# RWKV inverse: T and its transpose kept as sums in PSUM, seeded by a product with the unit matrix

## The reference, cut to what matters

```python
def _rwkv7_scan(r, w, k, v, a, b, s0):
    def step(s, inp):
        r_t, w_t, k_t, v_t, a_t, b_t = inp
        sa = jnp.einsum('bhvk,bhk->bhv', s, a_t)
        s = s * w_t[:, :, None, :] + sa[..., None] * b_t[:, :, None, :] + v_t[..., None] * k_t[:, :, None, :]
        o = jnp.einsum('bhvk,bhk->bhv', s, r_t)
        return s, o
```

## Time and profile before

| | |
|---|---|
| median of three executions | 2289.26 us |
| span of the profiled execution, first to last instruction | 2287.5 us |
| the three executions' own times | 2285.67, 2289.26, 2289.65 us |
| PE busy | 2230.2 us (97%) |
| DVE busy | 982.6 us (43%) |
| ACT busy | 421.9 us (18%) |
| POOL busy | 556.1 us (24%) |
| PE's share of the chain that ended last | 87% |

### The profile page before, as it was taken

How to read it: one execution, slowest core, us unless ns; L and a number is a source line. 1 busy time by engine, 2 the same in 40 slices (tenths; PEclk the granted TensorE clock), 3 DMA queues, 4 the chain that set the end, 5 groups by cost and what they waited for, 6 DMA issues and landing times.

```text
span 2287.5 us, 47135 instructions
## 1 busy us (share of the span) xinstructions
PE 2230.2 (97%) x20858; PEld 2105.6 (92%) x20858; DVE 982.6 (43%) x1259; ACT 421.9 (18%) x775; POOL 556.1 (24%) x288
## 2 busy tenths in 40 slices
PE   8999999999999999999999999999999999999998
PEld 6899988878888799889999988999999999999997
DVE  5333664747546355254443154445114314412523
ACT  4111313214141211163111032110000000000011
POOL 0232201111011022123333301333333333323331
PEclk9999999999999999999999999999999999999999
DMA  7211201112011083236113134111111111111112
GB/s 282 84 41 42 63 20 55 41 40 68 20 58 38 27 271 133 98 133 254 41 46 120 37 131 156 37 46 46 46 37 46 46 46 39 45 46 46 46 37 87
DMA packets 57711, 171.15 MB, mean 75 GB/s; under 512 B 8416, under 2 KB 24160, under 8 KB 54752
## 3 DMA queue, kind: packets, MB, share of 16 engines
q1 hardware_dynamic: 46816, 143.63, 19.0%
q10 hardware_dynamic: 10752, 25.35, 3.2%
HBM read 140.90 MB, written 28.05 MB: 74 GB/s over the span
## 4 chain that ended last, share of the span: by engine, by line
PE 87%; DVE 5%; DMA 3%; ACT 2%; issue 1%; SPq 1%; POOL 0%; ACTq 0%; DVEq 0%; POOLq 0%
PE ps L380 86%; DMA w_raw<-w 2%; DVE TT L1154 1%; DVE F L1154 1%; SPq L2219 1%; ACT F L1758 1%; DMA vc<-vc 1%; DVE F L1157 0%; DVE F L1160 0%; DVE Sst L1157 0%; ACT L1758 0%; DMA par<-par 0%; POOL w_split L371 0%; DVE Xst L1154 0%; PE ps L1024 0%
## 5 line engine op out<-in xcount | busy, mean ns | idle before, releaser
L380 PE MATMUL ps<-A_s,w_split 128*128 128x364 f32 (+1 forms) x6192 | 1081.6, 332 | 8.2 <-ACT zstg L1758 6.0
L380 PEld LDWEIGHTS ps<-A_s,w_split 128*128 128x128 f32 x6192 | 1029.3, 189 | 35.4 <-issue 12.2
L380 PE MATMUL ps<-B_s,w_split 128*128 128x364 f32 (+3 forms) x4032 | 672.5, 328 | 0.2 <-POOL w_split L371 0.2
L380 PEld LDWEIGHTS ps<-B_s,w_split 128*128 128x128 f32 x4032 | 667.7, 188 | 3.4 <-issue 1.0
L368 POOL CAST w_split<-w_raw 128x1024 fp32r<-128x1024 f32 x142 | 154.0, 1084 | 1685.6 <-PE ps L380 1599.7
L371 POOL TENSOR_TENSOR w_split<-w_raw,w_split 128x1024 fp32r<-128x1024 f32 x142 | 402.0, 2831 | 11.4
L1154 DVE TENSOR_TENSOR F<-ps,F 128x1092 f32<-128x1092 f32 (+3 forms) x52 | 62.8, 1208 | 420.6 <-PE ps L380 420.6
L1758 ACT ACTIVATE B_s<-T 128x1092 fp32r<-128x1092 f32 x32 | 35.9, 1121 | 621.6 <-DVE T L1160 621.6
L1160 DVE SCALAR_TENSOR_TENSOR T<-ps,rsx 128x1092 f32<-128x1092 f32 x32 | 41.5, 1296 | 205.3 <-PE ps L380 197.2
L1154 DVE TENSOR_TENSOR B_s<-T,B_s 128x1092 fp32r<-128x1092 f32 x32 | 105.9, 3309 | 1.1
L1154 DVE TENSOR_TENSOR T<-T 128x1092 f32<-128x1092 f32 x58 | 103.8, 1790 | 1.4 <-ACT T L1758 0.2
(11 more groups left out here) (208 smaller groups left out, 1806.0 us busy)
## 6 DMA issues: line engine op xcount, KB each, us to landing
w_raw<-w SPq DMA_DIRECT2D x144, 512.0 KB, 3.6
z<-zstg SPq DMA_DIRECT2D x83, 182.0 KB, 1.9
F<-z SPq DMA_DIRECT2D x16, 546.0 KB, 7.4
w_raw<-w SPq DMA_DIRECT2D x7, 1024.0 KB, 10.4
kc<-kc SPq DMA_DIRECT2D x7, 1024.0 KB, 4.8
vc<-vc SPq DMA_DIRECT2D x7, 1024.0 KB, 4.9
F<-x SPq DMA_DIRECT2D x8, 546.0 KB, 9.8
Zs<-z SPq DMA_DIRECT2D x16, 273.0 KB, 19.6
```

Of the source, the lines that this page charges most:

```text
L380: return pe.matmul(out, lhsT, rhs, start=start, stop=stop, skip_group_check=skip)
```

## The change

T and its transpose are no longer added up in SBUF. A new step `seed` multiplies both by the unit matrix into banks 3u and 3u+1 in level 1, and every level's product adds onto those sums in PSUM (`start=False`). After each level but the last, DVE copies T out of bank 3u (256 elements instead of 512, and no second operand), and ACT copies the transpose out of bank 3u+1 in every level. The next level's x waits for DVE's copy alone, its increments wait for ACT's too. The product `av` moves from level 1 to level 5 and lands in bank 3u, which is free by then; ACT's copy of it moves along. The mark "av" is gone, so ACT's copy of a finished piece of the gates comes behind the levels. DVE's add of the last level is gone, and `wu` waits for ACT's copy of the transpose and for `av_read`. The samples keep their code, with other counts in the waits (`at_t`) and one wait more in `wu`.

```diff
+            def seed(p, h, u):
+                b0 = 3 * u
+                pe.wait_ge(tk_ready, 2 * q_of(p, h) + 2)
+                for c in range(NB):
+                    cross(bank(b0, NB, C)[:, c, :], TT[u][:, 1, c, :], eye, start=(c == 0), stop=False, skip=True)
+                    last = cross(bank(b0 + 1, NB, C)[:, c, :], TT[u][:, 0, c, :], eye, start=(c == 0), stop=False, skip=True)
+                last.then_inc(lvt, 1)
+
+            def grow(p, h, u, lv):
+                b0 = 3 * u
+                pe.wait_ge(xst_ready, at_lv(p, h, lv))
+                pe.wait_ge(lvt, at_z(p, h, lv - 1))
+                for c in range(NB):
+                    if lv < LEVELS - 1:
+                        cross(bank(b0, NB, C)[:, c, :], TT[u][:, 1, c, :], Xst[u][:, c, :], start=False, stop=False, skip=True)
+                    last = both(bank(b0 + 1, NB, C)[:, c, :], Xst[u][:, c, :], TT[u][:, 1, c, :], start=False, stop=False, skip=True)
+                last.then_inc(yz_done, 1)
...
             def wu(p, h, u, nb, levels):
                 q, b0 = q_of(p, h), 3 * u
-                pe.wait_ge(lvl, at_lv(p, h, levels - 1))
+                pe.wait_ge(av_ready, q + 1)
+                if nb == NB:
+                    pe.wait_ge(lvt, at_z(p, h, levels - 1))
+                else:
+                    pe.wait_ge(lvl, at_t(p, h, levels - 1))
...
                     if lv == 1:
+                        for u in range(2):
+                            seed(p, 2 * g + u, u)
+                    if lv == LEVELS - 1:
                         for u in range(2):
                             av(p, 2 * g + u, u, NB)
-                        mark(p, g, "av")
                     for u in range(2):
-                        yz_level(p, 2 * g + u, u, NB, lv, LEVELS)
+                        grow(p, 2 * g + u, u, lv)
...
-                        for u in range(2):
-                            add_level(p, 2 * g + u, u, NB, lv, LEVELS)
+                        if lv < LEVELS - 1:
+                            for u in range(2):
+                                v.wait_ge(yz_done, at_lv(p, 2 * g + u, lv))
+                                v.tensor_copy(TT[u][:, 0, :, :], bank(3 * u, NB, C)).then_inc(lvl, 1)
...
+            def turned_level(p, h, u, lv):
+                a.wait_ge(yz_done, at_lv(p, h, lv))
+                act(TT[u][:, 1, :, :], bank(3 * u + 1, NB, C), ACT.Copy).then_inc(lvt, 1)
...
-                    reads(MARK[p, g, "av"])
-                    for u in range(2):
-                        av_read(p, 2 * g + u, u, NB)
+                    for lv in range(1, LEVELS):
+                        if lv == LEVELS - 1:
+                            for u in range(2):
+                                av_read(p, 2 * g + u, u, NB)
+                        for u in range(2):
+                            turned_level(p, 2 * g + u, u, lv)
```

More of the change, by code:

```diff
@@ L301, in hybrid_step @@
         d_s0r, d_rst, vm_ready, rs_done, rs_new = (sem(n) for n in ("d_s0r", "d_rst", "vm_ready", "rs_done", "rs_new"))
-        rn_mean, rn_ctr, rn_sq, rn_var, rn_rs, rn_out = (sem(n) for n in
-            ("rn_mean", "rn_ctr", "rn_sq", "rn_var", "rn_rs", "rn_out"))
+        rn_mean, rn_ctr, rn_sq, rn_var, rn_rs, lvt = (sem(n) for n in
+            ("rn_mean", "rn_ctr", "rn_sq", "rn_var", "rn_rs", "lvt"))
         rg_t, rg_f, rg_p, rg_hi, rg_s = (sem(n) for n in ("rg_t", "rg_f", "rg_p", "rg_hi", "rg_s"))
@@ L346, in at_lv, with at_t, at_z @@
             return n + h // 2 * 2 * (LEVELS - 1) + 2 * (lv - 1) + h % 2 + 1
+        def at_t(p, h, lv):
+            n = p * (HALVES * (LEVELS - 2) + SLEVELS - 1)
+            if h == HALVES:
+                return n + HALVES * (LEVELS - 2) + lv
+            return n + h // 2 * 2 * (LEVELS - 2) + 2 * (lv - 1) + h % 2 + 1
+        def at_z(p, h, lv):
+            return (2 * p + h // 2) * 2 * LEVELS + 2 * lv + h % 2 + 1
         NA = SEQ // P
@@ L595, in x_level @@
                 else:
-                    pe.wait_ge(lvl, at_lv(p, h, lv - 1))
+                    pe.wait_ge(lvl, at_t(p, h, lv - 1))
                 for c in range(nb):
@@ L602, in av @@
                 q, b0 = q_of(p, h), 3 * u
-                pe.wait_ge(tk_ready, 2 * q + 2)
+                if nb == 1:
+                    pe.wait_ge(tk_ready, 2 * q + 2)
                 for c in range(nb):
-                    last = cross(bank(b0 + 1, NB, C)[:, c, :], NAR[u][:, 1, c, 0:C], TK[u][:, 4, c, :])
+                    last = cross(bank(b0 + (0 if nb == NB else 1), NB, C)[:, c, :], NAR[u][:, 1, c, 0:C], TK[u][:, 4, c, :])
                 last.then_inc(av_done, 1)
+            def seed(p, h, u):
[14 more added lines that the diff above has]
+                last.then_inc(yz_done, 1)
             def yz_level(p, h, u, nb, lv, levels):
@@ L1298, in add_level @@
                 else:
-                    v.wait_ge(lvl, at_lv(p, h, lv - 1))
+                    v.wait_ge(lvl, at_t(p, h, lv - 1))
                 yz = ps[:, b0:b0 + 2, 0:NB * C].rearrange("p a (n c) -> p a n c", c=C)
@@ L1905, in av_read @@
                 a.wait_ge(av_done, q + 1)
-                act(TK[u][:, 1, 0:nb, :], bank(b0 + 1, NB, C)[:, 0:nb, :], ACT.Copy).then_inc(av_ready, 1)
+                act(TK[u][:, 1, 0:nb, :], bank(b0 + (0 if nb == NB else 1), NB, C)[:, 0:nb, :], ACT.Copy).then_inc(av_ready, 1)
+            def turned_level(p, h, u, lv):
+                a.wait_ge(yz_done, at_lv(p, h, lv))
+                act(TT[u][:, 1, :, :], bank(3 * u + 1, NB, C), ACT.Copy).then_inc(lvt, 1)
             def wu_read(p, h, u, nb):
```

## The result

| | before | after |
|---|---|---|
| median of the runs | 2289.45 us (2285.67 to 2292.88, 8 runs) | 2297.35 us (2292.88 to 2303.21, 8 runs) |
| ratio after/before, 95% interval | | 1.0041 [1.0031, 1.0051] |
| profiled execution, span | 2287.5 us | 2297.1 us |
| granted clock | 0.996 | 0.996 |

The changed kernel is slower by 0.4%, 8 to 10 us. Forecast were +2.6 us and most of the chance on "no difference that can be measured". The sign is the forecast's, the size is three times as large, and the time (2297.35) lies at the upper end of the range of 2284.5 to 2298, beside the slower rival's 2298.

What follows compares the result with a forecast made beforehand. PE was taken to bound the kernel, with the DVE-PE ring of 2.71 us bounding a level; -8.7 + 0.4 + 4.8 + 5.2 + 0.4 + 0.5 = +2.6 us gave 2291.9 us, range 2284.5 to 2298.

Steps and rivals of the forecast that it cites:

- slower rival: Levels 2 to 4: PE's queue bounds the rings, only 0.13 of 0.27 us gained in each; 2298 us, chance 0.20.
- Add becomes copy: Levels 1 to 4: DVE's 686 ns add becomes a 415 ns copy, 0.27 us less in each of 32 rings, -8.7 us.
- rings: One level's cycle of x, mask, increments and add or copy; 2.71 us before, forecast 2.44 in levels 2 to 4.
- ACT takes the transpose: Levels 1 to 4: ACT's 385 ns copy finishes over 1 us before the next increments need it; cost zero.
- the waits: Levels 1 to 4: increments wait for two semaphores instead of one; +0.4 us, bounded by 0 and 1.9.
- The seed: Level 1: 64 rows at 28 ns in av's place delay the increments, +0.6 us a group, +4.8 us in all.
- av to level 5: Level 5: av stands between x1 and the increments in PE's queue, +0.65 us a group, +5.2 us (0 to 7.2).
- the handover: Level 5: handing over from ACT to PE takes longer than from DVE, +0.05 us a group, +0.4 us.
- PE's own stalls: Levels 1 to 5: one 0.6 us stall a group shared over its rows makes the seed's extra rows cost +0.5 us.
- The faster rival: Levels 1 and 5: seed and av mostly fall into PE's 0.86 us of room in a level; 2284 us, chance 0.13.

Runs made afterwards that it cites:

- experiment 4: Kernel before with only av moved to level 5: ratio 0.9999; changed kernel without seed, DVE adding the unit matrix to x, av in level 1: 1.0002 to before.
- experiment 1: Changed kernel with the seed as two wide 128x128 unit-matrix products per part instead of sixteen of 64x64: 2287.12 us, ratio 1.0003 to the kernel before.
- experiment 2: Changed kernel with DVE copying both T and its transpose in levels 1 to 4, ACT only in level 5: 2296.12 us, 1.0047 to the kernel before.
- straight burst: Kernel before plus 1024 PE instructions (512 rows of 64x64 products) written straight ahead of the first pair: 2300.02 us, ratio 1.0057 to the kernel before.
- experiment 3: Kernel before plus 1024 PE instructions: straight ahead of the first pair 2300.02 us, there as a loop 2292.68, spread over the rings of levels 2 to 5 2297.13.
- looped rings: PE's levels 2 to 4 as a 3-pass loop in the before, changed and no-seed kernels: 1.0090, 1.0194, 1.0124 with small products; 1.0012, 1.0066, 1.0004 with semaphore increments.

## Why the prediction was wrong, by its steps

- **Add becomes copy, -8.7.** The step holds where PE isn't stopped: rings of 2.45 and 2.46, a copy's mean is 424 ns where 415 was taken. But from the first copy or add of level 1 to level 5's first mask the eight groups only went from 80.5 to 78.0 us, 2.5 less. The gain didn't come through in the changed kernel, nor in the version of experiment 4 without the seed, which is as slow as before. In experiment 1 it did: 9.5 us. So the term was right, and what took it away is below.
- **ACT takes the transpose, 0, and the waits, +0.4.** Right as far as can be seen: no row of PE's waits names ACT's copies of the transpose, and experiment 2 without ACT there takes the same time.
- **The seed, +4.8.** The time from first mask to first copy grew by 5.05 us over eight groups. As array time the size was right: without a stop the increments start 1.76 behind the seed, 0.55 more than the 1.21 of av; the rest is stops. The wide seed of experiment 1 costs 4.0 us at the same place. But the seed's larger price, its instructions, wasn't in the term.
- **av to level 5, +5.2, and the handover, +0.4.** Level 5 up to `G0T` grew by 7.6 us, and by 7.3 in experiment 1: these two terms were some 2 us too small. By itself the move makes no difference to the kernel (experiment 4: 0.9999), since level 1 gets shorter.
- **PE's own stalls, +0.5: the step that failed.** I had the rows, took them for accidents and shared out one stall of 0.6 a group in proportion to rows. (Even so the sum was off: 64/448 of 0.6 in eight groups is 0.7, and levels 1 to 5 have 480 rows with av.) They come from a limit on the instructions that reach PE in a stretch. PE's waits by issue rose from 3.2 to 11.5 us. What the term should have held is the difference between the changed kernel and experiment 1, which differ only in how the seed is written, by 896 instructions: 7.0 us from the first copy to level 5's mask and 1.0 ahead of it, some 9 us by the ratios, against the 0.5 forecast. At the straight burst's period of 3.74 us per 256 the estimate would be 13.1 us for 896 instructions if PE has nothing in hand; the runs that add 1024 cost 14.2 (straight) and 11.3 us (in the rings). The other terms, without this one, add up to +2.1; in experiment 1 they measure -9.5 + 4.0 + 7.3 = +1.8 by DVE's timelines, and the kernel is 1.3 longer by the medians. That those two sums lie so near is partly luck, since the copies gained 0.8 more, the seed cost 0.8 less and level 5 cost 1.7 more than forecast. It is luck too that the measured time lies inside the stated range: its upper end was the slower rival's, whose cause didn't happen.
- **The slower rival** had the place and nearly the price (2298), but its cause, parts 0.75 apart so that 1.85 of 2.44 us of issue don't fit, isn't what happened: the earlier trace rows's spacing went to about 0.5 and rings of 2.45 exist. **The faster rival** (2284) wanted the seed and av to vanish in PE's room; they show, with 5.05 and 7.6 us here and 4.0 and 7.3 in experiment 1.
- **What could have told.** A ring before uses 192 instructions in 2.71 us, 256 in 3.61, and the instruction queue on the page moves 2.02 MB in 123 packets, 16 KB each; in the groups of the kernel before they start 3.3 us apart at the least and mostly 3.3 to 4.0. The Trainium skill ("Runtime: NRT & Kernel Launch", section "Instruction fetch mechanics") says that instructions are fetched in blocks of 16 KiB, 256 of them, ahead of use, and that the crossing is mostly hidden. The block size agrees with the trace (33 GB/s for 0.5 us). That it is hidden doesn't: for fp32 products of 64x64 the straight burst shows 1.65 us of every 3.74 exposed, and the measurement decides.

Shown: that PE instructions in number, not array time, set the loss (experiments 1 and 3), and that the number ahead of the rings decides whether the shorter copy comes through: with the seed in 128 instructions a group it is worth 2.5 us, with the seed in 16 it is worth 9.5 (experiment 1), and in the changed kernel giving it up costs nothing (experiment 2). Argued only: how far the supply can get ahead in a stretch of few instructions, and so why the version without the seed has no gain left; and the looped rings, meant to show the limit lifted, brought costs of their own. No version beat the kernel before; the wide seed, the unit matrix in x and av alone in level 5 equal it.

## What to carry to other kernels

Count a change's TensorE instructions, weight loads too, not only its busy time. Straight code of small products (64x64 by 64 columns in fp32) is brought at some 3.7 us per 256 instructions here, which is slower than PE can do them, so a few wide products are cheaper than many small ones of equal array time. A ring of dependences that already uses 256 in 3.6 us gains from a faster copy only where the stretch ahead of it uses few instructions for its time, as with the wide seed. Stops by "issue" in the middle of a run of products are the sign of it: look how far apart they are, in instructions, before calling them noise.

## What the runs showed of the hardware that was not expected

- Straight small products: 128 rows in 2.09 us, then 1.42 to 1.65 us of nothing, period 3.74 us; 16 KB pieces in the instruction queue every 3.5 to 4 us in the groups.
- In no trace of these kernels do two pieces of the instruction queue start less than 3.2 us apart.
- The same 512 rows as a loop of 128 instructions: 8.95 us without a stop, and the kernel is 5.5 us longer than before instead of 14.2.
- Rings of 2.45, in three of the eight groups all three of them (576 instructions in 7.35 us), do run without a stop behind a seed that holds PE for 2 us with 16 instructions.
- A pass with waits on registers isn't free: up to 0.17 us a ring with four of them (2.88 against 2.71).
- A product of 128x128 by 8 columns between products of 64x64 takes 262 ns in its row, and four of them made a ring 0.9 us longer (masks 3.77 apart against 2.87 with increments in their place).
